# The low part of each weight unit made by an accumulating transfer instead of by VectorE, with squares and bias rows moved to VectorE and the loops written out

## The reference, cut to what matters

```python
def rmsnorm(x, g):
    y = x * lax.rsqrt(jnp.mean(x * x, axis=-1, keepdims=True) + NORM_EPS)
    return y * g

for i in range(2):
    h = rmsnorm(x, norm_mix[i])
    if i == 0:   # gate_b, gate_c, v = split(h @ w_in)
        x = x + (gate_b * conv3(gate_c * v)) @ w_out
    else:        # softmax(q k + bias over the window) v, per head
        x = x + neighborhood_attention_2d(h, w_qkv, rpb, w_o)
    h = rmsnorm(x, norm_mlp[i])
    a = jax.nn.relu(h @ w_up[i])          # 1024 -> 4096
    x = x + (a * a) @ w_down[i]           # 4096 -> 1024
return rmsnorm(x, norm_final)
```

## Time and profile before

| | |
|---|---|
| median of 3 runs | 1135.35 us |
| the profiled execution's own time | 1134.88 us |
| its span | 1133.3 us |
| granted TensorE clock, mean | 0.995 |
| TensorE busy | 1118.3 us (99%) |
| VectorE busy | 600.0 us (53%) |
| ScalarE busy | 353.8 us (31%) |
| GpSimd busy | 70.8 us (6%) |
| DMA, share of 16 engines | 31.8%, 108.54 MB |

### The profile page before, as it was taken

The page is one execution under the profiler, slowest core; times in us unless marked ns, Lnnn a source line. Parts: engine busy times, 40 slices in busy tenths (PEclk is TensorE's granted clock), DMA queues, the critical chain, the costliest instruction groups (busy, mean ns, idle before and its releaser), DMA issues.

```text
span 1133.3 us, 14288 instructions
## 1 busy us (share of the span) xinstructions
PE 1118.3 (99%) x5256; PEld 919.4 (81%) x5256; DVE 600.0 (53%) x945; ACT 353.8 (31%) x533; POOL 70.8 (6%) x60
## 2 busy tenths in 40 slices
PE   9999999999999999999999999999999999999995
PEld 8888888888888888888788878788888888888884
DVE  5856555734643543655565555566534634534633
ACT  6212342322322222233344454443212312212331
POOL 3000021000000000012010000121000000000020
PEclk9999999999999999999999999999999999999998
DMA  6336225336326332222221122122332322232211
GB/s 210 112 111 118 95 93 103 112 111 94 120 93 102 117 104 93 93 93 94 92 69 61 59 71 74 56 81 90 109 97 95 105 93 93 93 111 93 93 56 74
DMA packets 41324, 108.54 MB, mean 96 GB/s; under 512 B 8016, under 2 KB 14160, under 8 KB 41296
## 3 DMA queue, kind: packets, MB, share of 16 engines
q1 hardware_dynamic: 41296, 108.18, 31.8%
HBM read 106.07 MB, written 2.22 MB: 96 GB/s over the span
## 4 chain that ended last, share of the span: by engine, by line
PE 99%; DVE 1%; issue 0%; ACT 0%; POOL 0%; DVEq 0%; POOLq 0%
PE bank L306 31%; PE bank L308 30%; PE bank L307 30%; PE bank L421 1%; PE bank L406 1%; PE bank L393 1%; PE bank L352 1%; PE bank L354 1%; PE bank L353 1%; PE bank L431 1%; PE bank L324 0%; PE bank L343 0%; DVE shared L889 0%; PE bank L317 0%; DVE ev L667 0%
## 5 line engine op out<-in xcount | busy, mean ns | idle before, releaser
L306 PE MATMUL bank<-a_h,w_h 128*128 128x512 f32 x864 | 340.7, 394 | 0.8 <-DVE ev L682 0.8
L308 PE MATMUL bank<-a_h,w_l 128*128 128x512 f32 x864 | 336.6, 390 | 0.0
L307 PE MATMUL bank<-a_l,w_h 128*128 128x512 f32 x864 | 336.5, 389 | 0.0
L498 ACT ACTIVATE w_h<-raw 128x1024 fp32r<-128x1024 f32 x187 | 196.7, 1052 | 281.6 <-PE bank L308 278.6
L646 DVE TENSOR_TENSOR w_l<-raw,w_h 128x1024 fp32r<-128x1024 f32 x187 | 235.5, 1260 | 72.3 <-ACT w_h L498 68.5
L306 PE MATMUL bank<-h_h,w_h 128*128 128x512 f32 x640 | 249.8, 390 | 0.0
L308 PE MATMUL bank<-h_h,w_l 128*128 128x512 f32 x640 | 249.0, 389 | 0.0
L307 PE MATMUL bank<-h_l,w_h 128*128 128x512 f32 x640 | 249.0, 389 | 0.0
L306 PEld LDWEIGHTS bank<-a_h,w_h 128*128 128x128 f32 x864 | 162.2, 188 | 38.4 <-DVE ev L682 3.4
L308 PEld LDWEIGHTS bank<-a_h,w_l 128*128 128x128 f32 x864 | 162.2, 188 | 34.3
L307 PEld LDWEIGHTS bank<-a_l,w_h 128*128 128x128 f32 x864 | 162.3, 188 | 34.0 <-issue 1.0
(11 more groups left out here) (81 smaller groups left out, 493.2 us busy)
## 6 DMA issues: line engine op xcount, KB each, us to landing
raw<-weights SPq DMA_DIRECT2D x188, 512.0 KB, 3.3
bias<-bias_rows SPq DMA_DIRECT2D x48, 64.0 KB
xs<-x SPq DMA_DIRECT2D x8, 256.0 KB, 4.9
raw<-wave SPq DMA_DIRECT2D x8, 256.0 KB, 5.2
out<-shared SPq DMA_DIRECT2D x8, 256.0 KB, 2.4
bias_rows<-rpb SPq DMA_DIRECT2D x8, 15.5 KB, 4.3
par<-small SPq DMA_DIRECT2D x1, 32.0 KB, 1.8
```

Of the source, the lines that this page charges most:

```text
L306: nc.tensor.matmul(dense[bank][:], w_h[slot][:, k, :], hi[:, k, :], start=k == 0, stop=False)
L307: nc.tensor.matmul(dense[bank][:], w_h[slot][:, k, :], lo[:, k, :], start=False, stop=False)
L308: last = nc.tensor.matmul(dense[bank][:], w_l[slot][:, k, :], hi[:, k, :], start=False, stop=k == KT - 1)
L498: nc.scalar.activation(w_h[slot][:], raw[slot][:], ACT.Copy).then_inc(w_hi, 1)
```

## The change

The weight unit's low part is no longer computed by VectorE. ScalarE, which writes `w_h` as before, writes the negated rounding `-w_h` into `w_l` in a second instruction, and GpSimd issues a transfer from SBUF to SBUF that adds `raw` to it, so that `w_l = raw - w_h` once it has landed. TensorE waits for its semaphore (`lo_in`, one for each slot), and so does SP's next load into the slot's `raw`. Units 4 and 5 are still split by VectorE, and so is the wave of units 0 to 3. Units are split 3 ahead instead of 2, and `split_hi(v)` waits for `unit_done` at v - 3.

GpSimd's other work goes to VectorE: the sums of squares (`add_squares`; the first square is written into `ssq` itself, and no memset is left) and the copies of bias rows. All hardware loops on the engines are replaced by Python loops that write the instructions out; slots then follow `u % 4` in the attention too.

```diff
-AHEAD = 2
+AHEAD = 3
...
         @block.sync
...
+            def load(u):
+                slot, _ = landed(u)
+                if u < 10:
+                    sp.wait_ge(w_split, u - 3)
+                else:
+                    sp.wait_ge(lo_in[slot], rest_in(u - 4)[1])
+                sp.dma_start(raw[slot][:], weights[u].rearrange("p (k n) -> p k n", k=KT)).then_inc(raw_in[slot], 16)
...
         @block.gpsimd
...
-            def sum_squares(n):
...
-            def copy_bias(par_, head):
...
+            for u in range(6, U_END):
+                slot, _ = landed(u)
+                pool.wait_ge(w_neg, u - 5)
+                pool.dma_start(w_l[slot][:], raw[slot][:], accum_op=ALU.add).then_inc(lo_in[slot], 16)
...
         @block.tensor
...
-                pe.wait_ge(w_split, u + 1)
+                if u < 6:
+                    pe.wait_ge(w_split, u + 1)
+                else:
+                    pe.wait_ge(lo_in[slot], rest_in(u)[1])
...
-                with pe.Fori(start, count // 4) as i:
+                for i in range(start, count // 4):
...
         @block.scalar
...
-                act.wait_ge(raw_in[slot], count)
-                if vc >= 3 and not idle:
-                    act.wait_ge(unit_done, v - 2)
+                act.wait_ge(raw_in[slot], count)
+                act.wait_ge(unit_done, v - 3)
                 nc.scalar.activation(w_h[slot][:], raw[slot][:], ACT.Copy).then_inc(w_hi, 1)
+                if v > 5:
+                    nc.scalar.activation(w_l[slot][:], raw[slot][:], ACT.Copy, scale=-1.0).then_inc(w_neg, 1)
...
             for m in range(KT):
-                if m > 1:
+                if m:
                     split_hi(U_WO + m + AHEAD)
                 split_x(3, m)
...
         @block.vector
...
-            def split_lo(v, vc, i=0, per=4):
-                slot, _ = landed(vc, i, per)
-                dve.wait_ge(w_hi, v + 1)
-                nc.vector.tensor_tensor(w_l[slot][:], raw[slot][:], w_h[slot][:].bitcast(f32),
-                                        ALU.subtract).then_inc(w_split, 1)
...
+            def add_squares(n, m):
+                dve.wait_ge(sq_done, KT * n + m + 1)
+                if m > 1:
+                    dve.wait_ge(ssq_added, adds_before(n) + m - 1)
+                nc.vector.tensor_tensor(ssq, ssq, sq[m % 2], ALU.add).then_inc(ssq_added, 1)
...
+            def copy_bias(pair):
+                for par_ in range(2):
+                    nc.vector.tensor_copy(head_bias[par_], bias[:, 2 * pair + par_, :]).then_inc(bias_ready, 1)
```

More of the change, by code:

```diff
@@ L131, in encoder @@
         w_split = sem("w_split")
+        w_neg = sem("w_neg")
+        lo_in = [sem(f"lo_in{s}") for s in range(4)]
         unit_done = sem("unit_done")
@@ L181, in tap, with landed, rest_in @@
             return par[:, (5 + n) * KT + m:(5 + n) * KT + m + 1]
[L183 to L192, removed]
+        def landed(u):
+            return u % 4, 16 * (u // 4)
+        def rest_in(u):
+            return u % 4, 16 * (u // 4 - (1 if u % 4 < 2 else 0))
         X_FINAL = [None, U_OUT, U_ATT - KT, U_WO, U_END - KT]
@@ L199, in adds_before @@
         def adds_before(n):
-            return KT * n - min(n, 1)
+            return (KT - 1) * n
         @block.sync
         def _(sp):
[L205 to L211, removed]
+            def load(u):
[5 more added lines that the diff above has]
+                sp.dma_start(raw[slot][:], weights[u].rearrange("p (k n) -> p k n", k=KT)).then_inc(raw_in[slot], 16)
             sp.dma_start(par[:], small).then_inc(par_in, 16)
@@ L221, in _ @@
             for g in range(4):
-                with sp.Fori(4 * g + 1, 4 * g + 5) as i:
-                    for s in range(4):
-                        load(4 * i + s, 4 + s, i - 1)
+                for u in range(16 * g + 4, 16 * g + 20):
+                    load(u)
                 sp.wait_ge(rows_in, 16 * ROWS)
@@ L234, in _ @@
                         sp.dma_start(dst, src).then_inc(bias_in, 16)
[L235 to L243, removed]
+            for u in range(68, U_END):
+                load(u)
             for m in range(KT):
@@ L376, in mlp @@
                 chunk(0, norm)
-                with pe.Fori(1, CHUNKS) as c:
+                for c in range(1, CHUNKS):
                     chunk(c)
@@ L477, in _ @@
             pe.wait_ge(banks_zero, 3)
-            with pe.Fori(0, KT - 1) as j:
+            for j in range(KT - 1):
                 pair_step(j, 3 * j + (U_ATT + 3))
@@ L571, in mlp @@
                 chunk(0, first=True)
-                with act.Fori(1, CHUNKS - 1) as c:
+                for c in range(1, CHUNKS - 1):
                     chunk(c)
@@ L619, in _ @@
             for s in range(3):
-                split_hi(U_ATT + s + AHEAD, None, 0, 3)
+                split_hi(U_ATT + s + AHEAD)
                 if s == 0:
                     root(2)
-            with act.Fori(0, KT - 1) as j:
+            for j in range(KT - 1):
                 pair_step(j, 3 * j + (U_ATT + 3))
@@ L771, in chunk @@
                     for m in range(KT):
-                        if not (last and n == 1 and m >= KT - AHEAD):
-                            split_lo(u + (KT + m + AHEAD), mlp_start(n) + KT + m + AHEAD, i)
                         residual(u + (KT + m), m % 4, m)
@@ L776, in chunk @@
                             split_x(norm + 1, m)
+                        if last and m > 1:
+                            add_squares(norm + 1, m - 1)
                 chunk(0, first=True)
-                with dve.Fori(1, CHUNKS - 1) as c:
+                for c in range(1, CHUNKS - 1):
                     chunk(c)
                 chunk(CHUNKS - 1, last=True)
+                add_squares(norm + 1, KT - 1)
             for b in tposed:
@@ L854, in pair_step @@
                     take_q(u + 1)
-                    lo(2)
+                    copy_bias(pair + 1)
                 normalise(1, pair)
@@ L872, in _ @@
             take_k(U_ATT + 2, 2)
-            split_lo(U_ATT + 4, U_ATT + 4, 0, 3)
-            with dve.Fori(0, KT - 1) as j:
+            dve.wait_ge(bias_in, 16 * 3 * WIN)
+            copy_bias(0)
+            for j in range(KT - 1):
                 pair_step(j, 3 * j + (U_ATT + 3))
```

91 lines of the change are left out of this document (23 added, 68 removed).

## The result

The changed kernel takes 1140.42 us (median of 4 runs, 1139.47 to 1143.07), the kernel before in the same session 1135.25 us (4 runs, 1135.13 to 1135.42). The ratio is 1.0049, with a 95% interval of 1.0032 to 1.0067: slower by 5.2 us, 0.5%. The forecast was 1138.3 us in a range of 1135.5 to 1150, with slower at 0.72. The direction and the place that was named are right; the size at that place was too large, and a second place of about the same price was missed.

The account below looks back on a forecast made before the run. TensorE's matmuls were taken as the bound, busy 1118.3 of 1133.3 us. Terms of 0 steady state, +2.9 behind the attention, 0 at the MLPs and 0 elsewhere gave 1138.3 us against a median of 1135.35, range 1135.5 to 1150.

Parts of the forecast that it names:

- The step behind the attention: At `U_WO + 4`: split ends at 742.82 us, TensorE's turn is 745.60, L is 5.9, so +2.9 us.
- L: Time from the negation's end until TensorE can start: 5.9 us, from 3.3 landing, 1.3 second read, 1.3 GpSimd's step.
- rival 1: Quick transfer, no change: L under 5.3 us, GpSimd's step nearly free or the second read overlapping; chance 0.25.
- the steady state: Ordinary weight units: 12.8 us of room for L, hidden by 3 units of lead, cost 0.
- no others above 0.1 us: Sign in TensorE's waits: 2 to 4 us near 745 us, no others above 0.1 but those of before.
- Throughput: Per weight unit, transfer 2.6 us of the DMA engines, with the load 3.9 of 5.43 us, so it fits.
- rival 3: The stage is the bound: transfer with load exceeds 5.43 us, every unit waits; 1226 us at 6.0; chance 0.10.
- the DMA share up by 20 to 30 points: Sign in the changed profile: the DMA engines' busy share rises by 20 to 30 points.
- The MLPs' fifth units: At `U_MLP0 + 4`, likewise second MLP: split ends 199.24, TensorE arrives 206.13, 6.9 us left, cost 0.
- rival 2: Slow transfer: L between 6.9 and 13 us, both MLPs' fifth units late; 1145.6 us at 9; chance 0.17.
- Sums, bias rows, loops: VectorE's added sums and bias copies, exponentials 0.4 us later, written-out loops: all hidden, cost 0.
- rival 4: Written-out loops gain: 1134.3 us at best unless matmuls start closer; chance 0.03, with anything unseen.

Follow-up runs that it names:

- experiment 8: The changed kernel with a plain copy of `raw` into `w_l` in place of the adding transfer (low parts wrong): 1137.06 us, ratio 1.0021.
- experiment 3: The changed kernel with `U_WO + 4` split by VectorE as before, the other 185 transfers kept: 1141.42 us, ratio 1.0059.
- experiment 4: The changed kernel without its fourth burst of bias rows (a quarter of the bias missing): 1140.92 us, ratio 1.0055.
- experiment 5: The changed kernel without any burst of bias rows (no bias added): 1137.91 us, ratio 1.0026.
- experiment 6: The changed kernel with bias rows issued singly, four among every seven loads, and `U_WO + 4` and `+ 5` split by VectorE: 1134.98 us, ratio 0.9999.
- experiment 1: The kernel before with all twelve hardware loops written out, nothing else: 1135.29 us, ratio 1.0001.
- experiment 2: The kernel before with loops written out and sums of squares and bias copies on VectorE, which still makes all low parts: 1134.99 us, ratio 1.0000.

## Why the prediction was right, and where it was not

**The step behind the attention** held in every part but L. The unit can't be split before that point, the negation ended 3.43 us behind the predicted 742.82, where TensorE too was 3.5 us late, and TensorE then stood. The term was +2.9 us and measured +2.1. L was taken as 5.9 us and is 4.9: the part that was called the weakest, 1.3 us for a step of GpSimd's, is 0.28 us from the negation's end to the issue, and the issue's 0.9 us lies inside the landing's 4.54. The part for the second read was 1.3 us and measured 1.6 (4.54 less experiment 8's 2.91). By its L, under 5.3, this place alone was rival 1, the quick transfer. The Trainium skill, DMA: Bandwidth & Descriptors, anatomy of one DMA on the GpSimd path, gave the estimates of 3.2 us for a copy and 4.5 with a second read; the runs have 2.91 and 4.54, so it was nearer than the sum from rows. What made the total slower than that rival's is the next step.

**The step that failed** is "So I cost the steady state at nothing; the 3 units of lead hide it", and in it the sentence on the bursts. I asked how late the transfer would be and gave it 12.8 us of room, and both halves of that failed. A transfer beside a burst needs more: unit 65's landed after 13.8 us, and in experiments 3 and 4 such transfers took 14.1 to 14.8 us and cost 0.5 to 1.2 us each, although their loads were in time. And the room was counted from a split that begins when its slot comes free, while behind a burst it begins when the load lands. That load landed later against TensorE than before, and what follows it grew: 6.9 us of ScalarE and transfer where 1.1 + 1.2 us of ScalarE and VectorE stood. The earlier trace rows had the warning: one load of 14.6 us. I used it as a bound for L and never asked which unit had it and how much room that unit had left. The missing term measured 3.2 us in the profile (3.0 and 0.2) and 2.5 in the medians (experiment 5), and "no others above 0.1 us" was wrong by one wait of 2.8 us. Experiment 6 shows that spreading the rows removes it, at the same share of the DMA engines.

**Why the load landed later** was only in part tried. SP's twelve issues took 9.8 instead of 6.2 us, but they began earlier, and the load was issued at 356.18 us, 1.1 us before its time in the kernel before (357.26): the longer issuing isn't what made it late. From a burst's first issue to the landing of the load behind it, the four bursts took 17.9, 18.1, 21.0 and 21.1 us before, 22.6, 21.9, 25.3 and 26.0 us with the plain copies of experiment 8, and 25.7, 26.9, 28.0 and 30.1 us in the changed kernel. A copy takes about half the engines' time of an adding transfer, and it adds about half as much here. That points at the busy engines; it is one execution of each. A transfer beside a burst is another matter: a plain copy took 14.0 us there too, so its addition isn't what makes it late.

**Throughput.** 48.5% of 1138.8 us over 186 transfers is 2.97 us of the engines for one, where 2.6 was worked out; in experiment 8 a copy takes 1.57 us, a ratio of 1.9. The Trainium skill, Collectives: The Full Stack, section on the bandwidth ceiling, has an adding transfer at half a copy's rate; the runs agree. A load takes at most 1.7 us (experiment 5: 28.2% of 1137.5 us over 188, the queue's few other DMAs included), so transfer and load need 4.7 of 5.43 us instead of 3.9. It fits, and the second MLP shows no wait: rival 3 is wrong. But it leaves 0.7 us per unit to work off what a burst has delayed. The sign "the DMA share up by 20 to 30 points" was wrong: it rose from 31.8% to 79.3% (48.5 and 30.8), by 47.5 points, and the prediction's own 2.6 us for each of 186 transfers would have been 43.

**The MLPs' fifth units** were in time: the transfer of `U_MLP0 + 4` was issued at 199.71 us, where 199.24 was the predicted end of its negation, and no wait followed at the fifth unit of either MLP. Rival 2 is wrong.

**Sums, bias rows, loops** cost nothing (experiments 1 and 2), rival 4 gains nothing. VectorE came to 389.5 us and not to 410: the sixteen bias copies took 6.9 us and not 12.8, 27 sums came and not 31, and each split that went had taken 1.26 us and not 1.22. ScalarE came to 519.6 us and not to 550: a negation right behind its high part adds 0.96 us, and six table fetches of 1.28 us went. One small thing was overlooked: the exponentials of the first pair were to be 0.4 us later and were 1.6, for a table fetch of 1.28 us that the loops had kept elsewhere; 0.16 us in the profile, of which 0.1 stayed.

**The sum** was thus +2.9 with one term; in the profile it is +2.1 behind the attention, +3.2 at the fourth burst and +0.1 in the pairs of heads. Too much in one term and nothing in another partly cancelled. That the forecast of 1138.3 us came within 2.1 us of the measured time, and inside its range, is in part luck: the mechanism behind the attention was right, and it is less than half of the 5.2 us.

## What to carry to other kernels

When a stage of a pipeline is replaced by a slower one that is off the path, its lead over the consumer isn't the same for all units: look up the longest landing of the stage ahead, which unit it belongs to and how much room that unit had left before, and put the added latency there. A burst of small transfers in a load queue sets that lead, and it is better issued in single pieces among the loads. Taking work from an engine that isn't the bound gains nothing; here it made the low parts later at every place where the lead is short, and the best version found (experiment 6) only equals the kernel before.

## What the runs showed of the hardware

- An adding transfer from SBUF to SBUF of 128 x 4 KB takes 2.97 us of the 16 engines and at least 4.5 us from issue to landing, with 0.87 us of GpSimd for its issue; a plain copy takes 1.57, 2.8 and 0.53 us (the changed kernel, experiment 8).
- TensorE's clock can fall after a single wait of 2.0 us: in experiments 4 and 5 the matmuls behind it started 0.43 us apart for eight or nine of them, 1.6 us more than the wait itself. The changed kernel's profile has the same wait without that, and what decides it stays open.
- Twelve bias rows issued in one piece took SP 6.0 to 6.6 us without the transfers and 8.6 to 12.8 us with them beside; the load behind them landed after 11.5 to 14.6 and after 14.7 to 20.2 us. Issued one at a time among the loads (experiment 6), nothing took more than 8.9 us to land.
- Seven table fetches of ScalarE, 1.28 us each, became one when the loops were written out, and that one stood ahead of the exponentials (experiment 1).
